# Prompt attention of a hybrid decoder step: a longer lag between scores, transposes and weighted values, and the causal term as a matrix product

## The chip, the cores and the metric

One core of a Trainium2 chip runs the whole program. The metric is the device time of one execution in microseconds (us), lower is better. The profiler records one execution; its times are read as "us from the start of the span". TensorE (PE) does the matrix products and the transposes, VectorE (DVE) and ScalarE (ACT) read its results out of PSUM, GpSimd (POOL) and SyncE (SP, which issues the transfers) stand beside them.

## The reference

The program is one layer of a decoder for a prompt of 512 tokens and a group of 8 sequences of 8 sample tokens. The part that matters here is the prompt's latent attention with 8 heads:

```python
def mla_scores(qn, qp, kn, kp):
    s = jnp.einsum('bthd,bshd->bhts', qn, kn) + jnp.einsum('bthd,bsd->bhts', qp, kp)
    return s.astype(jnp.float32) * MLA_SCALE
...
        s = mla_scores(qn_i, qp_i, kn, kp)
        qpos = i * qb + jnp.arange(qb)
        s = jnp.where(kpos[None, :] <= qpos[:, None], s, -jnp.inf)
        p = jax.nn.softmax(s, axis=-1).astype(v.dtype)
        return jnp.einsum('bhts,bshd->bthd', p, v)
```

Scores of a query against all keys up to its own position, a softmax over them, and the weighted sum of the values. Everything is float32.

## The kernel before, in words

Each engine has its own instruction stream, and the streams meet through semaphores only. Between phases all of them meet at a barrier (`meet`, line 453). The phase in question begins behind `meet(..., 2)` and ends with `meet(..., 3)`; the sampled sequences' attention over their cached pages comes next.

The phase has 32 steps, one for each tile `t` of 128 queries (0 to 3) and head `h` (0 to 7), tile by tile. Step (t, h) works on (t + 1) * 128 keys, so a step of tile 3 has four times the keys of a step of tile 0. What one step does:

- PE, line 918: scores of 128 queries against (t + 1) * 128 keys, into one of three PSUM banks in turn. It first waits until the exponentials three steps back have left the bank (`reopen`, line 440). A float32 product stands in the trace as two records.
- DVE, line 1874: adds the causal term (0 or -1e30, a constant of 128 x 128 elements) to the last 128 columns, in PSUM, and waits for its own result (`link`); line 1875: the negated row maximum.
- ACT, line 1419: exponentials with the row maximum as bias and the row sum as second result (a second record), into `pr`, three buffers in SBUF.
- PE, line 925: t + 1 transposes of `pr` into one of two PSUM banks.
- Line 1881 (DVE, even steps) or line 1427 (ACT, odd steps): copies the transposed weights from PSUM into `prT`, two buffers. Both wait until the weighted values two steps back have used the buffer (`wait_prT_free`, line 491).
- PE, line 934: t + 1 products of a transposed block with the values (128 x 64), summed in a bank that the 8 heads of a tile share.

After the eighth head of a tile DVE takes the reciprocal of the row sums and scales the tile's output into `ot` (lines 1888 and 1891), PE transposes that (line 911, `out_rows`), and ACT copies it to `mixT` (line 1433).

The order is written out by hand: all three engines run the same loop over `n`, and each iteration takes the scores of step n, the transposes of step n - 2, the weighted values of step n - 3 and, where due, the output rows of the tile that ended at step n - 5. Within one iteration PE issues scores, transposes, weighted values in that order. DVE does the maximum of step n and then the copy of step n - 2; ACT does the exponentials of step n and then the copy of step n - 2, so that ACT's copy stands behind exponentials which wait for the newest scores.

SP meanwhile issues the loads of the first sequence's cached pages (lines 599 and 591), which the next phase reads; POOL prepares operands of the next phase and waits.

Of the kernel before, what the change touches and what calls it, by code (L numbers as in the profile page):

```python
# [24 lines left out]
ALU = mybir.AluOpType  # L25
ACT = mybir.ActivationFunctionType
AX = mybir.AxisListType

P = 128
# [13 lines left out]
MH, MV, ROPE = 8, 64, 32  # L43
MQ = MV + ROPE
# [199 lines left out]
PLAN, SEQ_STRIDE = make_plan()  # L244


def build(nc, x, xs, mem, consts, gains, rows, ring_w, w_kvb_d, w_kt_d, w_qb_d, w_a2_d, cache_ckv, cache_kpe,
          cache_mk, cache_mv, state, pages, y_p, y_s, ckv_p, kpe_p, mk_p, mv_p, gla_p, ckv_s, kpe_s,
          gla_s):
    with ExitStack() as ctx:  # L250
# [5 lines left out]
        def S(name):  # L256
            if name not in sems:
                sems[name] = ctx.enter_context(nc.semaphore(name))
            return sems[name]
# [6 lines left out]
        with ExitStack() as whole:  # L266
            hT = sb("hT", [P, KD * NT], extent=whole)
# [7 lines left out]
        with ExitStack() as before_mlp:  # L275
# [4 lines left out]
            stat = sb("stat", [P, 640], extent=before_mlp)  # L280
# [16 lines left out]
        def view(base, at, *shape):  # L297

            n = int(np.prod(shape))
            assert at + n <= base.shape[1], (at, shape)  # L300
            v = base[:, at:at + n]
            if len(shape) > 1:
                names = "abcd"[:len(shape)]
                v = v.rearrange(f"p ({' '.join(names)}) -> p {' '.join(names)}", **dict(zip(names, shape)))
            return v
# [6 lines left out]
        ident = cst[:, C_ID:C_ID + P]  # L312
        ones = cst[:, C_ONE:C_ONE + P]
        tri = cst[:, C_TRI:C_TRI + P]
        causal = cst[:, C_CAUS:C_CAUS + P]
# [47 lines left out]
        qT = view(arena, 4608, MH, TP)  # L363
# [15 lines left out]
        kT = view(arena, 0, MH, TP)  # L379
# [1 line left out]
        gq2 = view(arena, 22949, MV)  # L381
        gqr = view(arena, 23013, ROPE)

        pr = view(hT, 0, 3, 512)
        prT = view(hT, 1536, 2, 512)
        ot = view(hT, 2560, 2, 512)

        cpg = [view(arena, 17444, NPG, KR + 1), view(arena, 0, NPG, KR + 1)]
        kpg = [view(arena, 21556, NPG * ROPE), view(arena, 4112, NPG * ROPE)]
# [33 lines left out]
        bank_free = [S(f"bank_free{b}") for b in range(8)]  # L423
# [6 lines left out]
        def full(eng, key, turn=0, stride=0):  # L430

            b, n = at(key, turn, stride)
            eng.wait_ge(bank_full[b], n)
            return bank[b]
# [12 lines left out]
        def filled(ins, key):  # L447
            return ins.then_inc(bank_full[PLAN[key][0]], 1)
# [42 lines left out]
        def wait_prT_free(eng, n, steps):  # L491

            if n >= 2:
                t, h = steps[n - 2]
                if h < MH - 1:
                    eng.wait_ge(S("prT_used"), (n - 2) - t)
                else:
                    full(eng, ("po", t))
# [147 lines left out]
        def _(pe):  # L646
            mm, tr = nc.tensor.matmul, nc.tensor.transpose
# [27 lines left out]
            for j in range(4):  # L675
                o = reopen(pe, ("memT", j))
                for kk in range(2):
                    for t in range(2):
                        ins = tr(o[:, (kk * 2 + t) * P:(kk * 2 + t + 1) * P],
                                 memx[:, t, (2 * j + kk) * P:(2 * j + kk + 1) * P], ident)  # L680
# [16 lines left out]
            o = reopen(pe, "xTs")  # L697
            for k in range(KD):
                ins = tr(o[:, k * NS:(k + 1) * NS], xin_s[0:NS, k * P:(k + 1) * P], ident[0:NS, 0:NS])
            filled(ins, "xTs")  # L700
            for k in range(KD):
                o = reopen(pe, ("xT", k))
# [203 lines left out]
            def out_rows(t):  # L906

                pe.wait_ge(S("ot"), t + 1)
                o = reopen(pe, ("poT", t))
                for j in range(4):  # L910
                    ins = tr(o[:, j * P:(j + 1) * P], ot[:, t % 2, j * P:(j + 1) * P], ident)
                filled(ins, ("poT", t))

            for n in range(len(steps) + 5):
                if n < len(steps):
                    t, h = steps[n]
                    o = reopen(pe, ("s", t, h))
                    filled(mm(o[:, 0:(t + 1) * P], qT[0:MQ, h, t * P:(t + 1) * P], kT[0:MQ, h, 0:(t + 1) * P],  # L918
                              start=True, stop=True), ("s", t, h))
                if 2 <= n < len(steps) + 2:  # L920
                    t, h = steps[n - 2]
                    pe.wait_ge(S("pr"), n - 1)
                    o = reopen(pe, ("pT", t, h))
                    for s in range(t + 1):
                        ins = tr(o[:, s * P:(s + 1) * P], pr[:, (n - 2) % 3, s * P:(s + 1) * P], ident)
                    filled(ins, ("pT", t, h))
                if 3 <= n < len(steps) + 3:
                    t, h = steps[n - 3]
                    pe.wait_ge(S(f"prT{(n - 3) % 2}"), (n - 3) // 2 + 1)
                    if h == 0:  # L930
                        reopen(pe, ("po", t))
                    o = bank[PLAN[("po", t)][0]]
                    for s in range(t + 1):
                        ins = mm(o[:, h * MV:(h + 1) * MV], prT[:, (n - 3) % 2, s * P:(s + 1) * P],  # L934
                                 vp[:, s, h * MV:(h + 1) * MV], start=(s == 0), stop=(s == t))
                    if h < MH - 1:
                        ins.then_inc(S("prT_used"), 1)
                    else:
                        filled(ins, ("po", t))
                if n >= 5 and steps[n - 5][1] == MH - 1:  # L940
                    out_rows(steps[n - 5][0])
            meet(pe, 3)


# [292 lines left out]
        def _(act):  # L1237
# [171 lines left out]


            steps = [(t, h) for t in range(4) for h in range(MH)]
            for n in range(len(steps) + 5):
                if n < len(steps):
                    t, h = steps[n]
                    o = bank[PLAN[("s", t, h)][0]]
                    act.wait_ge(S("row_max"), n + 1)
                    if n >= 3:
                        full(act, ("pT", *steps[n - 3]))
                    A(pr[:, n % 3, 0:(t + 1) * P], o[:, 0:(t + 1) * P], ACT.Exp, bias=stat[:, 32 + n:33 + n],
                      accum_out=stat[:, 64 + n:65 + n]).then_inc(S("pr"), 1)  # L1420
                    act.wait_ge(S("pr"), n + 1)
                    act.nop().then_inc(bank_free[PLAN[("s", t, h)][0]], 1)
                if 2 <= n < len(steps) + 2 and n % 2 == 1:
                    t, h = steps[n - 2]
                    o = full(act, ("pT", t, h))
                    wait_prT_free(act, n - 2, steps)
                    nc.scalar.copy(prT[:, 1, 0:(t + 1) * P], o[:, 0:(t + 1) * P]).then_inc(S("prT1"), 1)
                    act.wait_ge(S("prT1"), (n - 2) // 2 + 1)
                    act.nop().then_inc(bank_free[PLAN[("pT", t, h)][0]], 1)
                if n >= 5 and steps[n - 5][1] == MH - 1:  # L1430
                    t = steps[n - 5][0]
                    o = full(act, ("poT", t))
                    freed(nc.scalar.copy(mixT[:, 4:8, t * P:(t + 1) * P], o[:, :].rearrange("p (j c) -> p j c", j=4)),
                          ("poT", t))
# [162 lines left out]
        def _(dve):  # L1597
# [269 lines left out]


            steps = [(t, h) for t in range(4) for h in range(MH)]
            for n in range(len(steps) + 5):  # L1870
                if n < len(steps):
                    t, h = steps[n]
                    o = full(dve, ("s", t, h))
                    link(V.tensor_tensor(o[:, t * P:(t + 1) * P], o[:, t * P:(t + 1) * P], causal, ALU.add))
                    V.tensor_reduce(stat[:, 32 + n:33 + n], o[:, 0:(t + 1) * P], AX.X, ALU.max, negate=True).then_inc(
                        S("row_max"), 1)
                if 2 <= n < len(steps) + 2 and n % 2 == 0:
                    t, h = steps[n - 2]
                    o = full(dve, ("pT", t, h))
                    wait_prT_free(dve, n - 2, steps)  # L1880
                    V.tensor_copy(prT[:, 0, 0:(t + 1) * P], o[:, 0:(t + 1) * P]).then_inc(S("prT0"), 1)
                    dve.wait_ge(S("prT0"), (n - 2) // 2 + 1)
                    dve.nop().then_inc(bank_free[PLAN[("pT", t, h)][0]], 1)
                if 4 <= n < len(steps) + 4 and steps[n - 4][1] == MH - 1:
                    t = steps[n - 4][0]
                    o = full(dve, ("po", t))
                    dve.wait_ge(S("pr"), 8 * t + 8)
                    link(V.reciprocal(stat[:, 0:8], stat[:, 64 + 8 * t:72 + 8 * t]))
                    if t >= 2:
                        full(dve, ("poT", t - 2))  # L1890
                    V.tensor_tensor(ot[:, t % 2, :].rearrange("p (h c) -> p h c", h=MH),
                                    o[:, :].rearrange("p (h c) -> p h c", h=MH), spread(stat[:, 0:8], 2, MV),
                                    ALU.mult).then_inc(S("ot"), 1)
                    dve.wait_ge(S("ot"), t + 1)
                    dve.nop().then_inc(bank_free[PLAN[("po", t)][0]], 1)
# [520 lines left out]
```

## Time and profile before

| | us |
|---|---|
| three runs: median (lowest to highest) | 1341.59 (1338.92 to 1341.65) |
| the profiled execution: its own time | 1340.34 |
| its span | 1338.5 |
| the phase of the 32 steps within the span | 339.5 to about 404.6 |

Busy time over the span, from the page:

| engine | busy us | share |
|---|---|---|
| PE (matmul records) | 1265.8 | 95% |
| PEld (weight loads) | 1085.6 | 81% |
| DVE | 606.1 | 45% |
| ACT | 380.6 | 28% |
| POOL | 258.2 | 19% |

A matmul record lasts from the issue of its first column to the modelled end of its last, and such records overlap each other; the start of one record to the start of the next is what a record costs the engine. The "idle before" of a group is time in which its engine stood still right ahead of it, with the instruction that ended the wait behind the arrow. PEclk is the granted TensorE clock: 1.00 is 2.4 GHz and 0.50 is 1.2 GHz.

### The profile page before, as it was taken

How to read it: one execution, taken by the hardware profiler on the slowest of the kernel's cores; microseconds unless marked ns; L12 is line 12 of the kernel's file. 1: busy time of each engine (PE TensorE's matmuls, PEld its weight loads, DVE VectorE, ACT ScalarE, POOL GpSimd, SP SyncE). 2: the span in 40 equal slices, each digit the busy share in tenths (PEclk: the TensorE clock that was granted, in tenths of full speed). 3: DMA queues.
4: the chain of work that ended last, by engine and by line, in shares of the span. 5: the costliest groups of instructions: out<-in, count | busy, mean ns of one | idle time of the engine just before them, and what ended most of it. 6: DMA issues, size and time to landing. Idle time of an engine off the chain costs nothing.

```text
span 1338.5 us, 21880 instructions
## 1 busy us (share of the span) xinstructions
PE 1265.8 (95%) x7851; PEld 1085.6 (81%) x7851; DVE 606.1 (45%) x1025; ACT 380.6 (28%) x852; POOL 258.2 (19%) x150
## 2 busy tenths in 40 slices
PE   7999998888899999999998998799999999999997
PEld 4665677645779999999996776469999999999997
DVE  1213033597554666656663215254445444444343
ACT  5011002342444454444440125523331001331000
POOL 0201030220104665565652120011000000000000
PEclk9999999598799999999999998899999999999999
DMA  9511040020201122221210621213222222222201
GB/s 341 206 47 32 0 157 16 13 60 0 68 5 49 33 71 69 70 70 51 60 33 1 238 77 32 95 32 100 90 79 79 79 83 90 80 78 80 78 0 71
DMA packets 60834, 97.39 MB, mean 73 GB/s; under 512 B 22961, under 2 KB 39506, under 8 KB 60690
## 3 DMA queue, kind: packets, MB, share of 16 engines
q1 hardware_dynamic: 59906, 93.51, 22.5%
q0 software_dynamic: 848, 2.89, 0.7%
q8 instruction: 41, 0.67, 0.2%
q14 instruction: 39, 0.32, 0.1%
HBM read 91.12 MB, written 5.25 MB: 72 GB/s over the span
## 4 chain that ended last, share of the span: by engine, by line
PE 77%; DVE 11%; ACT 3%; issue 3%; POOL 3%; DMA 2%; POOLq 0%; DVEq 0%; SPq 0%; ACTq 0%
PE bank L1197 31%; PE bank L667 14%; PE bank L753 4%; PE bank L1025 3%; PE bank L1027 3%; POOL stat L2283 3%; PE bank L1026 3%; PE bank L691 2%; PE bank L977 2%; PE bank L1053 2%; PE bank L957 1%; PE bank L934 1%; PE bank L918 1%; DMA arena<-in_cache_mk_dram 1%; DVE stat L1917 1%
## 5 line engine op out<-in xcount | busy, mean ns | idle before, releaser
L1197 PE MATMUL bank<-ur,wr 128*128 128x288 f32 x1536 | 205.3, 296 | 0.0
L1197 PE MATMUL bank<-hr,wr 128*128 128x288 f32 x1536 | 205.3, 296 | 0.0
L1197 PEld LDWEIGHTS bank<-ur,wr 128*128 128x128 f32 x1536 | 205.0, 189 | 0.1
L1197 PEld LDWEIGHTS bank<-hr,wr 128*128 128x128 f32 x1536 | 204.9, 189 | 0.1
L2283 POOL TENSOR_TENSOR stat<-stat,cst 128x32 f32<-128x32 f32 x32 | 173.7, 5428 | 2.5
L1025 PE MATMUL bank<-wq_high,c_parts 128*128 128x288 f32 x512 | 162.5, 317 | 2.9 <-ACT hT L1451 2.4
L1027 PE MATMUL bank<-wq_low,c_parts 128*128 128x288 f32 x512 | 151.5, 296 | 0.0
L1026 PE MATMUL bank<-wq_high,c_parts 128*128 128x288 f32 x512 | 150.9, 295 | 0.0
L2106 DVE CAST wr<-ring 128x1024 fp32r<-128x1024 f32 x64 | 44.5, 695 | 208.7 <-PE bank L1197 207.9
L667 PE MATMUL bank<-hT,ring 128*128 128x288 f32 (+1 forms) x512 | 125.7, 407 | 0.0
L1917 DVE TENSOR_REDUCE stat<-hT 128x8 f32<-128x512 f32 x128 | 86.9, 683 | 78.9 <-ACT hT L1451 74.4
L667 PEld LDWEIGHTS bank<-hT,ring 128*128 128x128 f32 (+1 forms) x512 | 93.9, 184 | 30.4 <-issue 1.2
L1025 PEld LDWEIGHTS bank<-wq_high,c_parts 128*128 128x128 f32 x512 | 96.7, 189 | 7.8 <-ACT hT L1451 3.8
L1026 PEld LDWEIGHTS bank<-wq_high,c_parts 128*128 128x128 f32 x512 | 97.0, 189 | 0.0
L1027 PEld LDWEIGHTS bank<-wq_low,c_parts 128*128 128x128 f32 x512 | 96.5, 189 | 0.0
L1576 ACT ACTIVATE hT<-bank 128x288 f32<-128x288 f32 x32 | 13.2, 412 | 234.3 <-PE bank L1197 234.3
L2108 DVE TENSOR_TENSOR wr<-ring,wr 128x1024 fp32r<-128x1024 f32 x64 | 78.5, 1226 | 2.2
L1451 ACT ACTIVATE hT<-bank 128x512 f32<-128x512 f32 x128 | 77.9, 608 | 0.8 <-DVE stat L1917 0.2
L1443 ACT COPY arena<-bank 128x64 f32<-128x64 f32 x128 | 27.3, 213 | 140.7 <-PE bank L1027 98.7
L753 PE MATMUL bank<-ring,hT 128*128 128x512 f32 (+3 forms) x160 | 53.1, 488 | 0.0
L753 PEld LDWEIGHTS bank<-ring,hT 128*128 128x128 f32 (+1 forms) x160 | 28.2, 179 | 23.2 <-issue 20.5
L1908 DVE TENSOR_TENSOR c_parts<-bank,c_parts 128x512 fp32r<-128x512 f32 x64 | 43.7, 683 | 6.6 <-ACT c_parts L1459 6.5
(370 smaller groups left out, 1650.3 us busy)
## 6 DMA issues: line engine op xcount, KB each, us to landing
ring<-in_ring_w_dram SPq DMA_DIRECT2D x106, 512.0 KB, 3.6
arena<-in_cache_ckv_dram SPq DMA_DIRECT2D x128, 128.0 KB, 2.0
arena<-in_cache_mk_dram SPq DMA_DIRECT2D x8, 512.0 KB, 3.8
arena<-in_cache_mv_dram SPq DMA_DIRECT2D x8, 512.0 KB, 8.9
mixT<-in_x_dram SPq DMA_DIRECT2D x1, 2048.0 KB, 13.2
arena<-in_cache_kpe_dram SPq DMA_DIRECT2D x128, 16.0 KB, 1.6
out_dram<-hT SPq DMA_DIRECT2D x4, 512.0 KB, 2.6
mixT<-in_w_qb_dram SPq DMA_DIRECT2D x1, 1152.0 KB, 13.3
```

The lines of the kernel that those rows point to most:

```text
L667: ins = mm(outs[c][0:m, 0:HALF], lhsT(k), src[:, k, c * HALF:(c + 1) * HALF], start=(k == 0), stop=(k == n_k - 1))
L753: ins = mm(o[0:m, 0:n_out], hTk[:, k, c0:c0 + m], ring[:, s0:s0 + n_out // P, k, :], start=(k == 0), stop=(k == KD - 1))
L1025: mm(o[:, 0:WQ - QH], c_parts[:, n % 2, 0, e, k, :], high, start=(k == 0), stop=False)
L1026: mm(o[:, 0:WQ - QH], c_parts[:, n % 2, 1, e, k, :], high, start=False, stop=False)
L1027: ins = mm(o[:, 0:WQ - QH], c_parts[:, n % 2, 0, e, k, :], low, start=False, stop=(k == KC - 1))
L1197: ins = mm(outs[c][:, 0:HALF], w[:, ew, k, :], src[:, ex, k0 + k, c * HALF:(c + 1) * HALF], start=(start and k == 0 and n == 0), stop=(sto ...
L1451: A(sqs[:, j % 2, :].rearrange("p (e c) -> p e c", e=2), o[:, :, keys_at:keys_at + WQ - 2 * QH], ACT.Square).then_inc(S("kr_free"), 1)
L1908: V.tensor_tensor(c_parts[:, n % 2, 1, :, :, :].rearrange("p e k c -> p (e k c)"), o[:, :], c_parts[:, n % 2, 0, :, :, :].rearrange("p e k ...
L1917: V.tensor_reduce(stat[:, 64 + 32 * g + 8 * (j % 4):72 + 32 * g + 8 * (j % 4)], sqs[:, j % 2, :].rearrange("p (h c) -> p h c", h=MH), AX.X ...
L2106: V.tensor_copy(wr[:, j % SPLITS, 0, :], src).then_inc(S("w_high"), 1)
L2108: V.tensor_tensor(wr[:, j % SPLITS, 1, :], src, wr[:, j % SPLITS, 0, :], ALU.subtract).then_inc(S("w_split"), 1)
L2283: G.tensor_tensor(r, r, power.broadcast_to([P, 32]), ALU.pow).then_inc(S("r_pg"), 1)
```

## The change

Four edits, all inside this phase:

1. The lags: transposes follow the scores by three steps (before: two), weighted values by four (before: three), output rows by six (before: five). The loops have one iteration more.
2. `pr` has four buffers (before: three); `prT` and `ot` move up in the same piece of SBUF.
3. ACT's copy of step n - 3 (the odd steps) is issued ahead of the exponentials of step n. DVE's copy still follows its maximum.
4. The causal term is no longer added by DVE: PE adds it as a product of the 128 x 128 identity with the causal constant, float32, into the last 128 columns of the scores' bank, right behind the scores.

```diff
-        pr = view(hT, 0, 3, 512)
-        prT = view(hT, 1536, 2, 512)
-        ot = view(hT, 2560, 2, 512)
+        pr = view(hT, 0, 4, 512)
+        prT = view(hT, 2048, 2, 512)
+        ot = view(hT, 3072, 2, 512)
...
-            for n in range(len(steps) + 5):
+            for n in range(len(steps) + 6):
                 if n < len(steps):
                     t, h = steps[n]
                     o = reopen(pe, ("s", t, h))
-                    filled(mm(o[:, 0:(t + 1) * P], qT[0:MQ, h, t * P:(t + 1) * P], kT[0:MQ, h, 0:(t + 1) * P],
-                              start=True, stop=True), ("s", t, h))
-                if 2 <= n < len(steps) + 2:
-                    t, h = steps[n - 2]
-                    pe.wait_ge(S("pr"), n - 1)
+                    mm(o[:, 0:(t + 1) * P], qT[0:MQ, h, t * P:(t + 1) * P], kT[0:MQ, h, 0:(t + 1) * P],
+                       start=True, stop=False, skip_group_check=True)
+                    filled(mm(o[:, t * P:(t + 1) * P], ident, causal, start=False, stop=True, skip_group_check=True),
+                           ("s", t, h))
+                if 3 <= n < len(steps) + 3:
+                    t, h = steps[n - 3]
+                    pe.wait_ge(S("pr"), n - 2)
                     o = reopen(pe, ("pT", t, h))
                     for s in range(t + 1):
-                        ins = tr(o[:, s * P:(s + 1) * P], pr[:, (n - 2) % 3, s * P:(s + 1) * P], ident)
+                        ins = tr(o[:, s * P:(s + 1) * P], pr[:, (n - 3) % 4, s * P:(s + 1) * P], ident)
                     filled(ins, ("pT", t, h))
-                if 3 <= n < len(steps) + 3:
-                    t, h = steps[n - 3]
-                    pe.wait_ge(S(f"prT{(n - 3) % 2}"), (n - 3) // 2 + 1)
+                if 4 <= n < len(steps) + 4:
+                    t, h = steps[n - 4]
+                    pe.wait_ge(S(f"prT{(n - 4) % 2}"), (n - 4) // 2 + 1)
...
-                if n >= 5 and steps[n - 5][1] == MH - 1:
-                    out_rows(steps[n - 5][0])
+                if n >= 6 and steps[n - 6][1] == MH - 1:
+                    out_rows(steps[n - 6][0])
...
+                if 3 <= n < len(steps) + 3 and (n - 3) % 2 == 1:
+                    t, h = steps[n - 3]
+                    o = full(act, ("pT", t, h))
+                    wait_prT_free(act, n - 3, steps)
+                    nc.scalar.copy(prT[:, 1, 0:(t + 1) * P], o[:, 0:(t + 1) * P]).then_inc(S("prT1"), 1)
...
                 if n < len(steps):
                     t, h = steps[n]
                     o = bank[PLAN[("s", t, h)][0]]
                     act.wait_ge(S("row_max"), n + 1)
-                    if n >= 3:
-                        full(act, ("pT", *steps[n - 3]))
-                    A(pr[:, n % 3, 0:(t + 1) * P], o[:, 0:(t + 1) * P], ACT.Exp, bias=stat[:, 32 + n:33 + n],
+                    if n >= 4:
+                        full(act, ("pT", *steps[n - 4]))
+                    A(pr[:, n % 4, 0:(t + 1) * P], o[:, 0:(t + 1) * P], ACT.Exp, bias=stat[:, 32 + n:33 + n],
                       accum_out=stat[:, 64 + n:65 + n]).then_inc(S("pr"), 1)
...
-                if 2 <= n < len(steps) + 2 and n % 2 == 1:
-                    t, h = steps[n - 2]
-                    o = full(act, ("pT", t, h))
-                    wait_prT_free(act, n - 2, steps)
-                    nc.scalar.copy(prT[:, 1, 0:(t + 1) * P], o[:, 0:(t + 1) * P]).then_inc(S("prT1"), 1)
...
                     o = full(dve, ("s", t, h))
-                    link(V.tensor_tensor(o[:, t * P:(t + 1) * P], o[:, t * P:(t + 1) * P], causal, ALU.add))
                     V.tensor_reduce(stat[:, 32 + n:33 + n], o[:, 0:(t + 1) * P], AX.X, ALU.max, negate=True).then_inc(
                         S("row_max"), 1)
-                if 2 <= n < len(steps) + 2 and n % 2 == 0:
-                    t, h = steps[n - 2]
+                if 3 <= n < len(steps) + 3 and (n - 3) % 2 == 0:
+                    t, h = steps[n - 3]
```

## Rows read from the trace of the kernel before

**Rows 1.** The page: the chain that ended last, shares by engine and line

```profile
PE 77%; DVE 11%; ACT 3%; issue 3%; POOL 3%; DMA 2%; POOLq 0%; DVEq 0%; SPq 0%; ACTq 0%
PE bank L1197 31%; PE bank L667 14%; PE bank L753 4%; PE bank L1025 3%; PE bank L1027 3%; POOL stat L2283 3%; PE bank L1026 3%; PE bank L691 2%; PE bank L977 2%; PE bank L1053 2%; PE bank L957 1%; PE bank L934 1%; PE bank L918 1%; DMA arena<-in_cache_mk_dram 1%; DVE stat L1917 1%
```

**Rows 2.** Busy time and granted clock by stretch; columns in the first line

```profile
core 0: us, PE busy (x) PEld busy (x) DVE busy (x) ACT busy (x) POOL busy (x), PEclk, DMA share, GB/s
339.50:404.60 65.10, 57.84 (x320) 44.79 (x320) 34.87 (x88) 29.02 (x84) 5.10 (x9) 0.87 0.14 37
...
340.57:343.98 3.41, 1.77 (x11) 1.35 (x12) 2.76 (x11) 2.23 (x10) 3.25 (x5) 1.00 0.34 90
...
344.00:361.00 17.00, 16.63 (x63) 13.68 (x63) 7.97 (x24) 6.90 (x26) 0.86 (x3) 0.50 0.38 108
361.00:404.60 43.60, 38.49 (x244) 28.99 (x242) 23.73 (x52) 19.87 (x50) 0.03 (x1) 1.00 0.04 6
```

**Rows 3.** Chain of waits, 393.50 to 398.21: start us, us, what (tile 3)

```profile
393.50 0.60 ACT hT L1427
...
394.14 1.10 PE bank L934 x8
395.24 0.93 PE bank L918 x2
...
396.19 0.31 DVE bank L1874
396.53 0.70 DVE stat L1875
...
397.26 0.79 ACT hT L1419 x2
...
398.21 0.59 ACT hT L1427
```

**Rows 4.** Waits of the phase: who waited for whom, us, times, longest

```profile
PEld bank L934 <- ACT hT L1427: 8.2, 13, 1.2
...
PE bank L934 <- ACT hT L1427: 4.4, 9, 1.0
```

**Rows 5.** PE in order of time, tiles 0 to 2

```profile
342.34 0.44 PE L918 MATMUL bank<-arena 96*128 96x128 f32 x2
342.62 0.27 PE L925 MATMUL bank<-cst,hT 128*128 128x128 f32 x1
...
361.92 0.65 PE L918 MATMUL bank<-arena 96*128 96x256 f32 x2
362.41 0.39 PE L925 MATMUL bank<-cst,hT 128*128 128x128 f32 x2
362.63 0.59 PE L934 MATMUL bank<-arena,hT 128*128 128x64 f32 x4
363.06 0.86 PE L918 MATMUL bank<-arena 96*128 96x384 f32 x2
363.76 0.39 PE L925 MATMUL bank<-cst,hT 128*128 128x128 f32 x2
```

**Rows 6.** PE in order of time, tile 3

```profile
391.72 1.00 PE L934 MATMUL bank<-arena,hT 128*128 128x64 f32 x8
392.56 1.08 PE L918 MATMUL bank<-arena 96*128 96x512 f32 x2
393.48 0.60 PE L925 MATMUL bank<-cst,hT 128*128 128x128 f32 x4
394.14 1.10 PE L934 MATMUL bank<-arena,hT 128*128 128x64 f32 x8
```

**Rows 7.** PE in order of time: 128-column float32 products at full and at half clock

```profile
204.84 3.74 PE L781 MATMUL bank<-arena 128*128 128x128 f32 x32
...
218.27 0.64 PE L801 MATMUL bank<-arena 128*128 128x128 f32 x2
218.70 0.63 PE L798 MATMUL bank<-hT,arena 128*128 128x128 f32 x2
```

**Rows 8.** The chain's end in this phase: start us, us, what

```profile
400.40 1.79 PE bank L934 x16
...
404.48 0.04 ACTq L456
```

**Rows 9.** ACT in order of time, tile 0

```profile
342.82 0.37 ACT L1419 ACTIVATE hT<-bank,stat 128x128 f32<-128x128 f32 x1 [0.35 <-DVE stat L1875]
343.09 0.19 ACT L1419 ACTIVATION_READ_ACCUMULATOR hT<-bank,stat 128x1 f32 x1
343.40 0.27 ACT L1427 COPY hT<-bank 128x128 f32<-128x128 f32 x1
343.85 0.37 ACT L1419 ACTIVATE hT<-bank,stat 128x128 f32<-128x128 f32 x1 [0.18 <-ACT hT L1427]
```

**Rows 10.** Groups of the phase by form: the causal add on DVE

```profile
L1874 DVE TENSOR_TENSOR bank<-bank,cst 128x128 f32<-128x128 f32 x32 | 9.6, 299 | 23.3 <-PE bank L918 22.8
```

**Rows 11.** Busy time by stretch (columns as in rows 2): when the page loads are through

```profile
358.00:378.00 20.00, 18.19 (x106) 14.10 (x105) 11.17 (x28) 9.65 (x27) 0.00 (x0) 0.92 0.11 21
378.00:404.50 26.50, 23.30 (x152) 17.51 (x150) 13.29 (x27) 11.38 (x26) 0.00 (x0) 1.00 0.00 1
```

More of the change, by code:

```diff
@@ L933, in _ @@
                     for s in range(t + 1):
-                        ins = mm(o[:, h * MV:(h + 1) * MV], prT[:, (n - 3) % 2, s * P:(s + 1) * P],
+                        ins = mm(o[:, h * MV:(h + 1) * MV], prT[:, (n - 4) % 2, s * P:(s + 1) * P],
                                  vp[:, s, h * MV:(h + 1) * MV], start=(s == 0), stop=(s == t))
@@ L1411, in _ @@
             steps = [(t, h) for t in range(4) for h in range(MH)]
-            for n in range(len(steps) + 5):
+            for n in range(len(steps) + 6):
+                if 3 <= n < len(steps) + 3 and (n - 3) % 2 == 1:
[3 more added lines that the diff above has]
+                    nc.scalar.copy(prT[:, 1, 0:(t + 1) * P], o[:, 0:(t + 1) * P]).then_inc(S("prT1"), 1)
+                    act.wait_ge(S("prT1"), (n - 3) // 2 + 1)
+                    act.nop().then_inc(bank_free[PLAN[("pT", t, h)][0]], 1)
                 if n < len(steps):
@@ L1422, in _ @@
                     act.nop().then_inc(bank_free[PLAN[("s", t, h)][0]], 1)
-                if 2 <= n < len(steps) + 2 and n % 2 == 1:
-                    t, h = steps[n - 2]
-                    o = full(act, ("pT", t, h))
-                    wait_prT_free(act, n - 2, steps)
-                    nc.scalar.copy(prT[:, 1, 0:(t + 1) * P], o[:, 0:(t + 1) * P]).then_inc(S("prT1"), 1)
[L1428 to L1431, printed above, removed]
+                if n >= 6 and steps[n - 6][1] == MH - 1:
+                    t = steps[n - 6][0]
                     o = full(act, ("poT", t))
@@ L1869, in _ @@
             steps = [(t, h) for t in range(4) for h in range(MH)]
-            for n in range(len(steps) + 5):
+            for n in range(len(steps) + 6):
                 if n < len(steps):
@@ L1873, in _ @@
                     o = full(dve, ("s", t, h))
-                    link(V.tensor_tensor(o[:, t * P:(t + 1) * P], o[:, t * P:(t + 1) * P], causal, ALU.add))
                     V.tensor_reduce(stat[:, 32 + n:33 + n], o[:, 0:(t + 1) * P], AX.X, ALU.max, negate=True).then_inc(
                         S("row_max"), 1)
-                if 2 <= n < len(steps) + 2 and n % 2 == 0:
-                    t, h = steps[n - 2]
+                if 3 <= n < len(steps) + 3 and (n - 3) % 2 == 0:
+                    t, h = steps[n - 3]
                     o = full(dve, ("pT", t, h))
-                    wait_prT_free(dve, n - 2, steps)
+                    wait_prT_free(dve, n - 3, steps)
                     V.tensor_copy(prT[:, 0, 0:(t + 1) * P], o[:, 0:(t + 1) * P]).then_inc(S("prT0"), 1)
-                    dve.wait_ge(S("prT0"), (n - 2) // 2 + 1)
+                    dve.wait_ge(S("prT0"), (n - 3) // 2 + 1)
                     dve.nop().then_inc(bank_free[PLAN[("pT", t, h)][0]], 1)
-                if 4 <= n < len(steps) + 4 and steps[n - 4][1] == MH - 1:
-                    t = steps[n - 4][0]
+                if 5 <= n < len(steps) + 5 and steps[n - 5][1] == MH - 1:
+                    t = steps[n - 5][0]
                     o = full(dve, ("po", t))
```

## The prediction

> **What bounds the kernel now.** I read the chain that ended last first: over the whole span it is mostly PE, and the lines of this phase hold 1% each [rows 1]. So the question is what happens inside one stretch of 65 us, and nothing outside it should move. The busy times by stretch give three facts [rows 2]. The phase lasts from 339.50 to about 404.5. PE's records cover 57.84 us of it. And TensorE ran at half clock (1.2 GHz, PEclk 0.50) from 344 to 361; before the fall, in the stretch 340.57 to 343.98, PE had been busy for only 1.77 us of 3.41 although its clock was full.
>
> The chain inside tile 3 shows the loop that sets the pace [rows 3]: ACT's copy of a transposed block (0.64 to the start of what waits for it), the weighted values (1.10), the next scores (0.95 to DVE's start), DVE's add (0.34 to the start of the maximum), the maximum (0.73 to the exponentials), the exponentials with their row sum (0.95 to the copy), and ACT's next copy. That is 4.71 us from copy to copy (393.50 to 398.21) and covers two steps. The loop exists because ACT's copy stands behind exponentials that need the newest scores. The waits say the same: the weighted values stood still for ACT's copy, 8.2 us by the weight loads and 4.4 us by the matmul records [rows 4].
>
> **PE's own work, at full clock, by start-to-start times.** Scores take 0.28 us with 128 columns (342.34 to 342.62), 0.49 with 256 (361.92 to 362.41), 0.70 with 384 (363.06 to 363.76) [rows 5] and 0.92 with 512 (392.56 to 393.48) [rows 6]; eight of each make 19.1. The weighted values take 0.84 for 8 records (391.72 to 392.56) [rows 6], so 160 records take 16.8. Two transposes take 0.22 (362.41 to 362.63) [rows 5], so one is 0.11 and four are 0.44 (in tile 3 the products behind them had waited, 393.48 to 394.14, so I don't take it there); 80 make 8.8, and 16 for the output rows 1.8. Sum: 46.5 us.
>
> The phase took 65.0. Of the difference, the half clock took about 8.5 (17.0 us in which PE's records fill 16.63, so nearly all of it is work that full clock would do in half the time) [rows 2]; the tail behind the last product 2.3 (400.40 + 1.79 to 404.48) [rows 8]; the remaining 7.7 are waits, most of them for ACT's copy [rows 4].
>
> **The change, part by part.**
>
> The *lags, the fourth buffer and ACT's order* go together. The copy of step n - 3 now needs transposes that PE issues right behind the scores of step n, and the weighted values of that step come a whole iteration later. In tile 3 an iteration of PE is over 2 us, and the copy takes 0.60 [rows 3, 6]: it is there long before. What is queued behind the copy on ACT is the exponentials of step n, which now also wait for PE's transposes of step n - 3. Who waits for those exponentials? The scores of step n + 3 (the bank) and the transposes at n + 3. The new loop in tile 3 is scores 0.92 and product 0.23, transposes 0.44, a handover of about 0.2, copy 0.60 and 0.18 to the next start [rows 9], exponentials 0.95: 3.5 us, for three iterations of 2.4 each. It does not bind. In tile 0 it is closer: ACT needs 0.58 from exponentials to the next instruction and 0.45 from copy to exponentials [rows 9], 1.6 for two steps or 0.81 a step, and PE needs 0.28 + 0.23 + 0.11 + 0.21 = 0.83. I leave 0.7 us of waiting for the filling (the fourth scores still wait for the first exponentials) and 0.9 for ragged spots, where ACT waits for the output rows: 1.6 in place of 7.7, so **-6.1 us** (bounds: all 7.7 gone; or 3 left, -4.7). The extra iteration adds no work; the tail (last weighted values, reciprocal, scaling, transposes, copy) is the same 2.3 [rows 8].
>
> The *product* adds 32 times identity by causal term, 128 x 128 in float32, two records each. The same form stands in the trace: 32 records in 3.74 us, 0.23 a pair, at full clock; 0.43 a pair at half clock (218.27 to 218.70) [rows 7]. With PE as the bound nothing hides it: 32 x 0.23 = **+7.4 us**. Bounds: 0.28 each by the 128-column scores, which carry the change of weights from another line [rows 5], 9.0 in all; and 0.43 each as the far end, 13.8. I take 0.23 since the form is the same.
>
> The *add* leaves DVE: 32 x 0.34 (299 ns each) [rows 10]. It was a link of the old loop; in the new one DVE is far from the bound, so beyond the waits already counted it is worth nothing. Its cover is PE's work: without the lags, removing it would shorten the loop by 0.34 and the product would give 0.23 back.
>
> The *clock*. It fell behind a stretch with PE half idle and rose at 361 [rows 2]. At full clock it has held through stretches with PE busy 38.49 of 43.60. The new kernel fills the early iterations: between 341 and 344 PE has about 0.83 us of work in each iteration of 0.85 to 0.9. I expect no fall: **-8.5 us** (bounds: 0, the same 17 us at half clock, or worse, see below).
>
> *Other queues.* SP's loads of the first sequence's pages are through by 378 (1 GB/s from there on) [rows 11], and the phase would end near 397, so they stay hidden; no load is moved. POOL only waits at the barrier. The next phase starts as a block, earlier.
>
> Sum: -6.1 + 7.4 - 8.5 = **-7.2 us**. The profiled execution took 1340.34, its span 1338.5; the median of the runs is 1341.59, 1.25 above. Against the median: 1334.4. Put another way, the phase would be 46.5 + 7.4 + 2.3 + 1.6 = 57.8 us long, and end at 397.3. Note the makeup: in tile 3 alone a step costs 2.36 now (4.71 / 2) and 2.43 after (0.92 + 0.23 + 0.44 + 0.84); the gain lies in tiles 0 to 2, and most of it in the clock.
>
> A measurement of this kernel can tell about 0.2% (2.7 us) from no change.
>
> **Rivals.**
>
> *A, slower: the clock falls again and stays down.* Place: tiles 0 and 1. For it: with float32 blocks this small, PE at half clock was busy 16.63 of 17.00 us and still took 17 us to rise [rows 2]; the product makes that stretch longer, since it costs 0.43 there [rows 7]. Against it: the cause of the fall, an idle PE before 344, is removed. Price: from 344 there are some 2 us of tile 0, 8 x 1.36 = 10.9 of tile 1 (0.49 + 0.23 + 0.22 + 0.42) and 0.4 of output rows left, 13.3 at full clock and 26.6 at half, so -7.2 + 13.3 = +6.1, 1347.7. It decides from 14.4 us at half clock on (no gain left), and from about 20 us on it is slower by 0.2%. Chance 0.11.
>
> *B, no change: the clock falls as before, for the same 17 us.* Its cause would be something the change does not touch. Then -6.1 + 7.4 = +1.3 us, 1342.9, within 0.2%. Against it stands that the idle PE is the only odd thing ahead of the fall [rows 2]. Chance 0.10. The Trainium skill, "TensorE: Matmul & The Clock Gate", section "Why this matters for your kernels", ties the drop of the clock to long idle gaps between bursts. By that rule the short waits here would not have lowered the clock, and B would hold. The same page, section "A second HAM failure mode: psum-queue depth-cycling", says that frequent micro-idles between groups make the clock swing, which is my forecast's side. The trace agrees with the second.
>
> *C, no change: PE is already full.* The records cover 57.84 of 65.10 us [rows 2]; the 7.3 left would be filled by the product's 7.4, 1341.6. Against it: a single record lasts 0.27 [rows 5] while 32 in a row start every 0.12 [rows 7], so records overlap and the idle time is larger than 7.3. Chance 0.06. The Trainium skill, "Perfetto Trace Analysis", section "Identifying the Most-Contended Engine", says matmul busy time is a poor measure of headroom and points to the weight loads' share instead. That is 44.79 of 65.10 here, 69%, which leaves room for the product; the trace agrees with the page.
>
> **How the numbers follow.** My forecast has 0.73. Its own range is 1332.8 (no waits left) to 1337.4 (3 us of waits left, the product at 0.28). A, B and C have 0.11, 0.10 and 0.06. Faster by over 0.2%: 0.73; within: 0.10 + 0.06 = 0.16; slower: 0.11. The range for 8 in 10 takes my forecast with the runs' own spread at its foot (1338.92 to 1341.65 before), and most of B and C: 1330.5 to 1343.
>
> **What would show it.** Right: the phase is near 58 us; PEclk reads 1.00 from 340 to 361; the wait of the weighted values for ACT's copy is gone; a step of tile 3 repeats every 2.4 us or so; PE's waits sit in tile 0. Wrong: PEclk 0.50 in tiles 0 and 1 (A, B); the gap between the scores and the transposes grows by more than 0.3 (product dearer); ACT's exponentials or copies late for PE in tile 0, with waits over 3 us in all.

## The result, and the profile after

The changed kernel takes 1330.29 us (median of 4 runs, 1328.94 to 1331.82) against 1341.47 for the kernel before (1338.92 to 1341.65): 0.9921 of it, with a 95% interval of 0.9903 to 0.9939. Forecast were 1334.4 us and "faster"; the direction is right, the gain was 11.2 us by the medians where I gave 7.2. A second set of 4 runs, beside 7 of the kernel before, gave 1330.69 and 0.9922 (0.9904 to 0.9941). The two profiled spans differ by 9.2 us (1338.5 and 1329.3).

That difference comes from the phase. By the phase I mean the time from the first scores' record to the end of ACT's last copy into `mixT`: 339.53 to 404.48 before, 339.50 to 394.93 after, 64.95 and 55.43 us. What stands ahead of it is equal (both begin at 339.5), what stands behind it takes 934.0 and 934.3: the phase is 9.5 us shorter, the rest 0.3 longer. Busy times by stretch of the changed kernel (columns as in rows 2):

```profile
339.40:395.00 55.60, 53.62 (x384) 46.44 (x384) 25.51 (x57) 28.82 (x84) 5.06 (x8) 1.00 0.17 44
339.40:344.00 4.60, 4.34 (x34) 4.02 (x35) 2.14 (x9) 2.55 (x11) 4.24 (x6) 1.00 0.21 65
344.00:361.00 17.00, 17.00 (x124) 15.40 (x123) 8.39 (x23) 10.68 (x36) 0.82 (x3) 1.00 0.39 110
361.00:395.00 34.00, 32.29 (x231) 27.03 (x229) 14.98 (x27) 15.59 (x37) 0.00 (x0) 1.00 0.05 8
```

PEclk is 1.00 throughout. Where the kernel before ran 63 records at half clock between 344 and 361 [rows 2], the changed one runs 124 in the same 17 us. The waits of the phase, longest first (POOL's waits for the barrier left out):

```profile
DVE stat L1876 <- PE bank L920: 24.2, 30, 1.7
ACT hT L1428 <- DVE stat L1876: 10.9, 13, 1.9
ACT hT L1419 <- PE bank L927: 9.5, 13, 2.0
PEld bank L920 <- issue: 3.8, 16, 0.2
```

The wait of the weighted values for ACT's copy [rows 4] has no successor here; it is DVE and ACT that wait for PE now. In the filling of the pipeline (PE in order of time) one short wait is left, 0.16 us for the bank that the first exponentials free:

```profile
339.50 0.49 PE L918 MATMUL bank<-arena 96*128 96x128 f32 x2 [0.88 <-DVEq L456]
339.83 0.39 PE L920 MATMUL bank<-cst 128*128 128x128 f32 x2
340.05 0.39 PE L918 MATMUL bank<-arena 96*128 96x128 f32 x2
...
341.27 0.49 PE L918 MATMUL bank<-arena 96*128 96x128 f32 x2 [0.16 <-ACTq L1431]
341.60 0.39 PE L920 MATMUL bank<-cst 128*128 128x128 f32 x2
341.82 0.27 PE L927 MATMUL bank<-cst,hT 128*128 128x128 f32 x1
```

Product to the next record is 0.22 us (339.83 to 340.05). And the chain at the end of the phase, which answers to rows 3 and 8:

```profile
387.00 0.84 PE bank L936 x8
387.85 0.44 PE bank L927 x4
...
390.85 1.79 PE bank L936 x16
392.67 0.21 DVE stat L1889
392.91 0.70 DVE hT L1892
...
393.65 0.67 PE bank L911 x4
394.35 0.58 ACT mixT L1435
```

From the fourth scores (341.27) to the last weighted values (392.64) the chain is PE alone. Ahead of that it leaves PE once, for about a microsecond (340.23 to 341.27): through DVE's first maximum and ACT's first exponentials. The tail behind it is 2.3 us, as before.

### The profile page after: what moved, and what is told of

It reads as the page before. It is cut to its first block, busy times and chain, and to the rows that moved or that the text cites. A ratio compares the mean times of both kernels' runs of the same rounds, so it can differ in the third digit from the quotient of the medians.

```text
span 1329.3 us, 21975 instructions
## 1 busy us (share of the span) xinstructions
PE 1260.2 (95%) x7915; PEld 1086.6 (82%) x7915; DVE 596.5 (45%) x993; ACT 380.1 (29%) x852; POOL 258.0 (19%) x150
## 4 chain that ended last, share of the span: by engine, by line
PE 79%; DVE 10%; POOL 3%; issue 3%; ACT 2%; DMA 2%; POOLq 0%; DVEq 0%; SPq 0%; ACTq 0%
PE bank L1199 31%; PE bank L667 14%; PE bank L753 4%; PE bank L1027 3%; PE bank L1029 3%; POOL stat L2284 3%; PE bank L1028 3%; PE bank L979 2%; PE bank L691 2%; PE bank L1055 2%; PE bank L918 1%; PE bank L936 1%; PE bank L959 1%; DVE stat L1918 1%; DMA arena<-in_cache_mk_dram 1%
## 5 line engine op out<-in xcount | busy, mean ns | idle before, releaser
L753 PE MATMUL bank<-ring,hT 128*128 128x512 f32 (+3 forms) x160 | 53.1, 489 | 0.0
```

Of the source, the lines that this page charges most:

```text
L753: ins = mm(o[0:m, 0:n_out], hTk[:, k, c0:c0 + m], ring[:, s0:s0 + n_out // P, k, :], start=(k == 0), stop=(k == KD - 1))
```

## The experiments

Two theories were open. Mine had three terms: the waits go (-6.1), the product costs (+7.4), the clock no longer falls (-8.5). It left open which of the edits removes the waits (the order of ACT, or the longer lags with the fourth buffer), and whether the clock needs the product's work. The rivals say that the lags do it, that the product is only a cost, or that the fall of the clock has another cause. Each run below has one profile; "half clock" is the time at PEclk 0.50 within the phase of that profile.

| kernel | ACT's copy first | lags of 3 and 4, four buffers | product | phase, us | half clock, us | median, us |
|---|---|---|---|---|---|---|
| before | no | no | none | 64.95 | 17.1 | 1341 to 1343 |
| filler | no | no | none; 20 unread products | 61.41 | 0.0 | 1337.27 |
| product_only | no | no | all tiles | 59.93 | 0.4 | 1335.26 |
| order_back | no | yes | all tiles | 59.71 | 0.4 | 1336.61 |
| order_only | yes | no | none | 54.41 | 10.2 | 1333.29 |
| lags_add | yes | yes | none | 55.09 | 10.2 | 1332.09 |
| order_product | yes | no | all tiles | 55.41 | 0.0 | 1331.89 |
| the change | yes | yes | all tiles | 55.43 | 0.0 | 1330.29 |
| product_twice | yes | yes | all tiles, twice | 61.79 | 0.0 | 1340.09 |
| product_tile0 | yes | yes | tile 0 | 51.80 | 0.1 | 1327.26 |
| order_product_tile0 | yes | no | tile 0 | 51.57 | 0.0 | 1328.87 |

The kernel before ran beside each set, with medians of 1342.5 (15 runs), 1341.43 (19) and 1341.15 (7). The phase is the sharper measure: outside it single executions differ by some us (the phase begins between 337.9 and 342.5 us in these traces).

One trace per kernel could be a chance one. The mean granted clock of the other executions, over the whole program, says that it isn't for the fall of the clock: 17.1 us at half clock take 0.0064 off that mean, and it is 0.962 in the median for the kernel before (0.958 to 0.968, 41 executions) and 0.968 for the change (0.967 to 0.969, 8 executions). Six of the 41 read 0.965 or more, so in a few the fall may have been shorter or absent.

**lags_add: the change without the product.**

```diff
-                    mm(o[:, 0:(t + 1) * P], qT[0:MQ, h, t * P:(t + 1) * P], kT[0:MQ, h, 0:(t + 1) * P],
-                       start=True, stop=False, skip_group_check=True)
-                    filled(mm(o[:, t * P:(t + 1) * P], ident, causal, start=False, stop=True, skip_group_check=True),
-                           ("s", t, h))
+                    filled(mm(o[:, 0:(t + 1) * P], qT[0:MQ, h, t * P:(t + 1) * P], kT[0:MQ, h, 0:(t + 1) * P],
+                              start=True, stop=True), ("s", t, h))
...
+                    link(V.tensor_tensor(o[:, t * P:(t + 1) * P], o[:, t * P:(t + 1) * P], causal, ALU.add))
```

> The changed kernel, but DVE adds the causal term again and PE does no product for it. My account (PE bound, the product costs its 0.23 us in each of 32 steps, the order of ACT frees the loop): the phase is 46 + 2.3 us and up to 3 us of waits in tile 0, 49 to 51.5 against 55.5 in the changed kernel, so about 5 us faster than it, 1325. Rival (the product's extra work on PE is what keeps the clock at full in tiles 0 and 1): the clock falls to half there again, and the phase is 56 us or longer, no faster than the changed kernel.

1332.09 us (ratio 0.9938, 0.9917 to 0.9959), phase 55.09. Busy times by stretch (columns as in rows 2):

```profile
339.50:344.00 4.50, 3.34 (x21) 2.59 (x22) 3.45 (x13) 2.56 (x11) 4.25 (x6) 0.99 0.23 72
344.00:350.00 6.00, 6.00 (x23) 4.83 (x22) 3.33 (x12) 3.04 (x12) 0.79 (x3) 0.50 0.39 112
350.00:356.00 6.00, 6.00 (x32) 5.30 (x31) 4.24 (x12) 2.51 (x9) 0.00 (x0) 0.66 0.41 122
```

The rival was right here. With 3.34 us of PE's records in the first 4.5 (4.34 of 4.60 with the product) the clock falls at 344, for 10.2 us. The 49 to 51.5 us of my account did not come. At half clock about 5 us are lost; leaving out 32 products of 0.22 us should have saved 7, and the phase is only 0.3 us shorter than the changed kernel's. The other 1.7 us or so must be waits and gaps of PE; of its waits the matmul records show 0.9 us for a bank and 0.2 for DVE's copy, both in the first 4.5 us. So the product pays for itself only by keeping PE occupied.

**product_only: the kernel before with the product in place of DVE's add.**

```diff
-                    filled(mm(o[:, 0:(t + 1) * P], qT[0:MQ, h, t * P:(t + 1) * P], kT[0:MQ, h, 0:(t + 1) * P],
-                              start=True, stop=True), ("s", t, h))
+                    mm(o[:, 0:(t + 1) * P], qT[0:MQ, h, t * P:(t + 1) * P], kT[0:MQ, h, 0:(t + 1) * P],
+                       start=True, stop=False, skip_group_check=True)
+                    filled(mm(o[:, t * P:(t + 1) * P], ident, causal, start=False, stop=True, skip_group_check=True),
+                           ("s", t, h))
...
-                    link(V.tensor_tensor(o[:, t * P:(t + 1) * P], o[:, t * P:(t + 1) * P], causal, ALU.add))
```

> The kernel before with the product in place of DVE's add and nothing else. My account: the loop over ACT's copy stays; it loses DVE's link (0.34) and gains the product (0.23), so the waits stay, and the phase is 59 to 60 us if the clock stays full, about 66 if it falls as before (1 us slower than the kernel before). Rival (the product's work alone keeps the clock full and is the main gain): about 1336, half of the change's gain.

1335.26 us (0.9948, 0.9931 to 0.9964), phase 59.93, half clock 0.4 us. 32 products more on the busiest engine, and the phase is 5.0 us shorter, because 17.1 us at half clock became 0.4. That is the rival's outcome in size; the length is the 59 to 60 that I gave for a clock that stays full.

**filler: the kernel before with useless work on PE.**

```diff
                     filled(ins, ("pT", t, h))
+                    if n < 12:
+                        for _ in range(2):
+                            mm(bank[7][:, 0:P], ident, causal, start=True, stop=True)
```

> The kernel before, lags, order and DVE's add as they were, with useless work on PE: in the iterations 0 to 11 two products of identity and causal term into a PSUM bank that nobody reads, in the place where PE waits for ACT's copy. If PE's idle time in tile 0 is what lowers the clock: the clock stays full through tiles 0 and 1, and the phase shrinks from 65 to 59 to 61 us although 20 products are added; about 1337. Rival (the fall has another cause): the half clock stays for 10 to 17 us, the phase is 66 us or longer.

1337.27 us (0.9975, 0.9956 to 0.9994), phase 61.41. The stretch of tiles 0 and 1, and two of its waits:

```profile
344.00:361.00 17.00, 15.72 (x110) 13.38 (x109) 10.50 (x33) 8.77 (x32) 0.97 (x3) 1.00 0.39 110
```

```profile
PEld bank L937 <- ACT hT L1430: 7.5, 14, 1.2
...
PE bank L937 <- ACT hT L1430: 4.1, 9, 1.0
```

Over the phase PE's waits for ACT's copy are nearly those of before (7.5 and 4.1 against 8.2 and 4.4 [rows 4]). Most of them lie behind 361. The one wait of this kind in tile 0 ahead of 344 is gone from the matmul records; in the kernel before it was

```profile
343.72 0.45 PE L934 MATMUL bank<-arena,hT 128*128 128x64 f32 x2 [0.82 <-ACT hT L1427]
```

and the unread products stand in its place. What also stays is the wait of 0.9 us for the first exponentials. PE's records fill 3.45 of the first 4.35 us of the phase, against 2.72 of 4.50 before. 20 products that nobody reads shorten the phase by 3.5 us. This is the cleanest sign for the clock's cause: too little work on PE in tile 0.

**order_only: the kernel before with ACT's copy put first.**

```diff
             for n in range(len(steps) + 5):
+                if 2 <= n < len(steps) + 2 and n % 2 == 1:
+                    t, h = steps[n - 2]
+                    o = full(act, ("pT", t, h))
...
                 if n < len(steps):
                     t, h = steps[n]
                     o = bank[PLAN[("s", t, h)][0]]
                     act.wait_ge(S("row_max"), n + 1)
...
-                if 2 <= n < len(steps) + 2 and n % 2 == 1:
-                    t, h = steps[n - 2]
-                    o = full(act, ("pT", t, h))
```

> The kernel before, with ACT's copy put ahead of its exponentials and nothing else (lags, buffers and DVE's add as they were). If the order alone breaks the loop, the phase is as short as with the longer lags and the add, 50 to 52 us, or 58 to 59 if the clock falls. Rival (the longer lags are what breaks the loop): with the lag of two steps the weighted values still wait, and the phase stays above 60 us, within 0.3% of the kernel before.

1333.29 us (0.9933, 0.9909 to 0.9957), phase 54.41 with 10.2 us at half clock. Moving one block in one engine's program, with lags, buffers and DVE's add untouched, shortens the phase by 10.5 us: the lag of two steps was no hindrance. It is neither of the two lengths that I gave (50 to 52, or 58 to 59 with a fall): the half clock is shorter than the 17.1 us of before. The two largest waits among PE, ACT and DVE are those of ACT for DVE and of DVE for PE; PE's weighted values have a single wait for ACT left, of 0.2 us by the weight loads (PE's longest, 0.9 us in the matmul records, is that of the first transposes for the first exponentials):

```profile
ACT hT L1426 <- DVE stat L1875: 16.2, 24, 2.1
DVE bank L1874 <- PE bank L918: 12.4, 22, 1.2
```

**order_back: the change with ACT's copy behind the exponentials again;** lags, buffers and product stay.

```diff
-                if 3 <= n < len(steps) + 3 and (n - 3) % 2 == 1:
-                    t, h = steps[n - 3]
-                    o = full(act, ("pT", t, h))
...
                 if n < len(steps):
                     t, h = steps[n]
...
+                if 3 <= n < len(steps) + 3 and (n - 3) % 2 == 1:
+                    t, h = steps[n - 3]
+                    o = full(act, ("pT", t, h))
```

> The changed kernel with ACT's copy of step n - 3 put behind the exponentials of step n again; lags, four buffers and product stay. If the order breaks the loop: the waits for ACT's copy come back, a step costs more than PE's work, and the phase is 59 us at full clock or 65 if it falls, 3 to 10 us slower than the changed kernel. Rival (the lags do it): same as the changed kernel, 55.5 us, 1330.

1336.61 us (0.9962, 0.9943 to 0.9981), phase 59.71 at full clock, 4.3 us longer than the change. Its waits:

```profile
PEld bank L936 <- ACT hT L1429: 4.0, 8, 0.7
...
PE bank L936 <- ACT hT L1429: 1.8, 5, 0.5
```

The weighted values wait for ACT's copy again, with the long lags. And the phase is that of product_only (59.93), which has the short lags: the lags do nothing in this pair.

**order_product: the change without the longer lags and the fourth buffer,** that is, the edits of order_only and of product_only together. Against the change:

```diff
-        pr = view(hT, 0, 4, 512)
+        pr = view(hT, 0, 3, 512)
...
-                if 3 <= n < len(steps) + 3:
-                    t, h = steps[n - 3]
-                    pe.wait_ge(S("pr"), n - 2)
+                if 2 <= n < len(steps) + 2:
+                    t, h = steps[n - 2]
+                    pe.wait_ge(S("pr"), n - 1)
```

> ACT's copy ahead of its exponentials and the product on PE, with the old lags and three buffers: the changed kernel without the longer lags. If the lags are worth nothing once the order is changed: clock full, phase 55.5 to 56.5 us, same as the changed kernel, 1331. Rival (PE bound by the product, the lag of two steps is too short): waits of PE for ACT's copy come back, the phase is over 58 us.

1331.89 us (0.9930, 0.9906 to 0.9953), phase 55.41 against 55.43: no difference in this pair either.

**product_twice: the change with every product done twice** (the masked scores then hold -2e30).

```diff
+                    mm(o[:, t * P:(t + 1) * P], ident, causal, start=False, stop=False, skip_group_check=True)
                     filled(mm(o[:, t * P:(t + 1) * P], ident, causal, start=False, stop=True, skip_group_check=True),
```

> The changed kernel with each product of the causal term done twice (the masked scores then hold -2e30). If PE sets the pace in every tile, each further product shows in full: 32 x 0.23 = 7.4 us more, phase 62.5 to 63, about 1338. Rival (part of the product is hidden in waits of PE): clearly less than 6 us more.

1340.09 us (0.9995, 0.9985 to 1.0005), phase 61.79, 6.4 us above the change. PE in order of time, tile 3:

```profile
387.23 1.02 PE L918 MATMUL bank<-arena 96*128 96x512 f32 x2
388.09 0.38 PE L920 MATMUL bank<-cst 128*128 128x128 f32 x2
388.31 0.39 PE L921 MATMUL bank<-cst 128*128 128x128 f32 x2
388.53 0.60 PE L928 MATMUL bank<-cst,hT 128*128 128x128 f32 x4
```

Each of the two takes 0.22 us (0.224 to a digit more, 7.2 for 32). From the first scores of one tile to the first of the next it is 1.79 and 1.78 us more than in the change for tiles 1 and 2, where eight products are 1.79, but only 1.00 more for tile 0: that is where the missing 0.8 lies. So PE is the bound from tile 1 on, and the phase stays 0.7 us below the 62.5 that I expected at least.

**product_tile0: the product in tile 0 alone.**

```diff
-                    mm(o[:, 0:(t + 1) * P], qT[0:MQ, h, t * P:(t + 1) * P], kT[0:MQ, h, 0:(t + 1) * P],
-                       start=True, stop=False, skip_group_check=True)
-                    filled(mm(o[:, t * P:(t + 1) * P], ident, causal, start=False, stop=True, skip_group_check=True),
-                           ("s", t, h))
+                    ins = mm(o[:, 0:(t + 1) * P], qT[0:MQ, h, t * P:(t + 1) * P], kT[0:MQ, h, 0:(t + 1) * P],
+                             start=True, stop=t > 0, skip_group_check=True)
+                    if t == 0:
+                        ins = mm(o[:, 0:P], ident, causal, start=False, stop=True, skip_group_check=True)
+                    filled(ins, ("s", t, h))
...
+                    if t > 0:
+                        link(V.tensor_tensor(o[:, t * P:(t + 1) * P], o[:, t * P:(t + 1) * P], causal, ALU.add))
```

> The changed kernel with the product in tile 0 alone; in tiles 1 to 3 DVE adds the causal term. In tile 0 ACT sets the pace (0.81 us a step against 0.60 of PE without the product), so 8 products cost nothing there and fill PE; in the other tiles 24 x 0.23 = 5.5 us of PE go. My account: the clock stays full, the phase is 50 to 51.5 us, 4 to 5 us below the changed kernel, about 1326. Rival (it takes the product in tile 1 too to hold the clock): a stretch of half clock begins in tile 1 and the phase is 54 to 56 us, no better than the changed kernel.

1327.26 us (0.9896, 0.9873 to 0.9920; four runs, 1326.97 to 1327.40), phase 51.80. This version beats both kernels, the changed one by about 3 us in the median and 3.6 in the phase (I had expected 4 to 5). Busy times by stretch:

```profile
339.50:344.00 4.50, 4.34 (x38) 4.02 (x37) 2.18 (x9) 2.79 (x12) 4.25 (x7) 1.00 0.29 87
344.00:350.00 6.00, 5.96 (x39) 4.62 (x38) 4.47 (x14) 4.19 (x18) 0.46 (x2) 1.00 0.39 112
350.00:356.00 6.00, 5.96 (x39) 4.82 (x39) 4.79 (x13) 3.86 (x12) 0.00 (x0) 1.00 0.41 116
```

In the first 4.5 us PE is as full as in the change, and from tile 1 on its own work (scores, transposes, weighted values) holds the clock without the product. The 24 products left out are 5.3 us of PE's work, and the phase is 3.6 us shorter: some waits of PE are back, among them the weighted values for DVE's copy, which now stands behind an add:

```profile
PEld bank L937 <- DVE hT L1885: 1.0, 4, 0.3
```

The 1.7 us that are missing lie mostly in tile 1: from its first scores to the first of tile 2 it takes 9.74 us in the change and 9.34 here, though eight products are 1.8 us. In tile 0 both take 5.85; in tile 2, 14.11 and 12.39, the products come off nearly in full. What holds PE back in tile 1, beyond the waits named, no run here shows.

**order_product_tile0: the same with the short lags,** run beside the change itself (changed_again, no edit). Its edit against order_only:

```diff
+                    if t == 0:
+                        ins = mm(o[:, 0:P], ident, causal, start=False, stop=True, skip_group_check=True)
...
-                    link(V.tensor_tensor(o[:, t * P:(t + 1) * P], o[:, t * P:(t + 1) * P], causal, ALU.add))
+                    if t > 0:
+                        link(V.tensor_tensor(o[:, t * P:(t + 1) * P], o[:, t * P:(t + 1) * P], causal, ALU.add))
```

> The changed kernel itself, a second time, beside the next one: 1330 to 1332, phase 55.5 us with the clock full throughout.

> ACT's copy ahead of its exponentials, the product in tile 0 alone, DVE's add in tiles 1 to 3, and the old lags with three buffers. If the longer lags are worth nothing: phase 51.5 to 52.5 us at full clock, 1327 to 1328, same as with them (51.80, 1327.26). Rival (without the product PE is fast enough in tiles 1 to 3 for the shorter lag to show): waits of PE for ACT's copy, phase over 53.5 us.

changed_again: 1330.69 us, phase 55.42. order_product_tile0: 1328.87 us (0.9897, 0.9876 to 0.9919; 1324.79 to 1329.95), phase 51.57 against 51.80 with the long lags. The median lies 0.9 us above the 1328 that I gave as the upper end, within the scatter of the four. A third pair in which the lags make no difference.

## Why the prediction was right, and where it was off

*What bounds it.* Right. The loop over ACT's copy set the pace [rows 3, 4], and PE's own work took over. The new phase should have been PE's 46.5 + 7.4 us, plus the tail of 2.3 and 1.6 for waits: 57.8, ending at 397.3. It is 55.4, so the sum was 2.4 us too long. PE's stretch from 339.50 to 392.64 is 53.1 us, against 53.9 of work and 1.6 of waits by my sum. The work was too large by about 1.5: 0.44 for the last tile's output rows, which I had counted in the tail as well; 0.2 to 0.3 for the product at 0.224; 0.6 for the weighted values, which take 0.17, 0.39 and 0.62 us for 2, 4 and 6 records where I had spread tile 3's price over them (0.21, 0.42, 0.63); and small change in the scores. The other step that was mis-sized is the **allowance for waits in tile 0**. Of 1.6 us about half was used: the fourth scores start 0.33 us late (0.55 us behind a product that takes 0.22; 0.16 by the records), and the other gaps between PE's groups there are about 0.1 us and less each. I had put PE's 0.83 us a step beside ACT's 0.81 and taken that for ragged; the trace shows the two running side by side.

*The order of ACT, the lags and the buffer.* I costed them as one edit, -6.1 us, and that was too coarse a step. The gain belongs to the order alone: with the product in place and the clock full it is worth 4.3 us (order_back) or 4.5 (product_only to order_product), less than the 6.1 of my term, while the product in the old order was worth more than its terms said (7.4 us of products and the 8.5 of the clock would leave 1.1; it was 5.0, DVE's add being gone from the loop as well). The terms are right in sign and add up nearly, but each depends on what else is changed. Three pairs that differ only in the lags and the fourth buffer are equal within 0.3 us: 59.93 and 59.71, 55.41 and 55.43, 51.57 and 51.80. In a fourth, without any product, the long lags are 0.7 us longer (order_only 54.41, lags_add 55.09), in one trace each. The ratios to the kernel before show no gain either, within their intervals: 0.9948 and 0.9962, 0.9930 and 0.9921, 0.9897 and 0.9896, 0.9933 and 0.9938. My loop for tile 3 (3.5 us for three iterations) already said that the new order has much room to spare; asked of the old lags, it would have given the answer.

*The product.* Its price was right: 0.22 us where I took 0.23, confirmed by doing it twice. That the clock and the product together (-8.5 and +7.4) come out slightly negative, as forecast, hides that the product itself holds the clock. I had written that filling "the early iterations" would prevent the fall, and meant waits gone as much as product added. The runs part them: with the new order but no product, the clock still fell for 10.2 us (order_only, lags_add); with the product and the old order it stayed full (product_only). So the product is the cause of the full clock, and of a gain of 5.0 us in the old order and of about nothing in the new one (54.41 and 55.09 without it, 55.4 with it; by the medians, 1333.29 and 1332.09 without it, 1331.89 and 1330.29 with it, it may be 1 to 2 us).

*The clock.* That it would stay at full was right, and my estimate of its worth, half of 17.1 us, is 8.5. The filler puts an upper bound beside it: 3.5 us gained and at most 20 x 0.224 = 4.5 spent make at most 8.0. Rival A and rival B (it falls again, for longer or as long) did not occur. B's ground, a cause that the change does not touch, is refuted by the filler: 20 products on PE in tiles 0 and 1, with nothing else changed, keep the clock up. The Trainium skill, "TensorE: Matmul & The Clock Gate", section "A second HAM failure mode: psum-queue depth-cycling", describes such a swing from small idle times between groups, and the trace agrees in part: the longest wait for ACT's copy was 1.2 us [rows 4] and the clock was down for 17.1, but the filler kept a wait of 0.9 us in tile 0 and its clock stayed full. The table of the same page of the Trainium skill in "Why this matters for your kernels", which speaks of long gaps between bursts, would not have foreseen it.

*Rival C* (PE already full) is out: 320 records covered 57.84 of 65.10 us [rows 2], and 384 now fit into 55.60.

*From the phase to the median.* The profiled executions differ by 9.2 us and the medians by 11.2, or 10.5 in the second set. The kernel before spreads over 1336.88 to 1346.92 in the runs of this study, so one profile of it can lie a microsecond or two off its median. I did not resolve this part further. Nor is it settled why the half clock lasts 10.2 us with the new order and 17.1 with the old; each is seen in one or two traces.

## What to carry to other kernels

Before lengthening a software pipeline, look at what stands ahead of the late instruction on its own engine: here moving one copy ahead of exponentials that wait for the newest data did all that lags and a further buffer were meant to do. Where the engine with the clock is idle part of the time at the head of a phase, give it work there even at the price of more instructions, and only there: the product in tile 0 was enough to keep the clock, and in the other tiles it cost 3.6 us net. When an edit adds work to the bound engine and the kernel still gets faster, run it with the work and without the rest of the change; two opposite effects had nearly cancelled in this one, 7 us of products against 5 us lost at half clock and some 2 of waits and gaps.

## What the runs showed of the hardware that was not expected

- 20 products whose results nobody reads made the kernel before faster (1337.27 against 1341.43 us, ratio 0.9975, 0.9956 to 0.9994): the granted clock stayed at 2.4 GHz from 344 to 361 in place of 1.2.
- The clock fell even where PE's records filled 3.34 of 4.50 us ahead of the fall (lags_add), and stayed full with 4.34 of 4.50 (product_tile0). The filler is close to the first of these: 3.45 of 4.35, and the clock stayed full. So the time that the records fill doesn't by itself tell the two cases apart here.
- A float32 product of 128 x 128 x 128 that accumulates onto columns just written by the product before it costs no more than an independent one: 0.22 us against 0.23 at most [rows 7].
